# The rest of the modulation summed on VectorE from weights laid out by columns

## The chip, the cores and the metric

The kernel runs on one core of one Trainium2 chip. The metric is the device time of one execution in microseconds (us). Before the change it is 3389.24 us, the median of three runs (3387.71 to 3394.56).

## What is computed

Two transformer-like blocks, all in float32. The first block has two layers over 256 latent and 256 context tokens of width 2048. The layers (`DEPTH` is 2) hold four groups of attention (`oa` to `od`). What the change touches is the modulation at the head of each layer: from two condition vectors `c` and `c_ctx` come a shift, a scale and a gate of 2048 each, by one product with `w_mod[l]` (2048 x 6144).

```python
def first_block(x, c, ctx, c_ctx, w_mod, b_mod, pre_norm_g, w_in, ...):
    silu_c = jax.nn.silu(c)
    silu_cc = jax.nn.silu(c_ctx)
    h, hc = x, ctx
    for l in range(DEPTH):
        with_ctx = l < DEPTH - 1
        shift, scale, gate = jnp.split(silu_c @ w_mod[l] + b_mod[l], 3, axis=-1)
        shift_c, scale_c, gate_c = jnp.split(silu_cc @ w_mod[l] + b_mod[l], 3, axis=-1)
        n = rms_norm(h, pre_norm_g[l]) * (1.0 + scale[:, None]) + shift[:, None]
        nc = rms_norm(hc, pre_norm_g[l]) * (1.0 + scale_c) + shift_c
        p = jnp.split(n @ w_in[l], split_points, axis=-1)
        pc = jnp.split(nc @ w_in[l], split_points, axis=-1)
...
        y = (jnp.concatenate([oa, ob, on, od], axis=-1) * jax.nn.silu(p[12])) @ w_out[l]
        h = h + gate[:, None] * rms_norm(y, post_norm_g[l])
        if with_ctx:
            yc = (jnp.concatenate([oa_c, ob_c, on_c, od_c], axis=-1) * jax.nn.silu(pc[12])) @ w_out[l]
            hc = hc + gate_c * rms_norm(yc, post_norm_g[l])
    return h
```

The second layer needs no gate for the context. The second block (a state-space mixer beside latent attention, then a feed-forward part) is not touched.

## The kernel before

The program is written out by hand: a class `Order` makes one list of steps, and each of the five engines' programs (SyncE, ScalarE, GpSimd, VectorE, TensorE) goes through this list and issues its own part of each step. So every engine works in the order of the list, and semaphores tie the parts together. Nothing is reordered later.

**Projections.** `project` multiplies tiles of 128 tokens by 512 columns of a weight matrix. Weights come in pieces of 128 x 1024 (two slices of 128 rows) through a ring of three on SyncE's queue (line 2409). Each piece is split in two float32r parts: ScalarE copies the high part (`high`, line 1884), VectorE subtracts it for the low part (`low`, line 1227). TensorE makes three products per slice and tile (lines 906 to 908) in `products`. With four token tiles a piece is 24 products; a projection has eight pieces. After each slice and tile of products `side()` is called: one tick of a clock by which other work is put between the products (transposes of heads, one step of attention), and on every fourth tick one step of the background. So a piece has eight ticks and two background steps. The first layer has 1152 ticks.

**Modulation.** The shift and scale of the first layer are made at the start, on TensorE (`mod_products`, line 923, and `mod_turn`), and stay there. The rest, 4 column chunks of 512 of the first layer's gate and 12 of the second layer, is the background generator `modulation()`, and all of it runs during the first layer. For each chunk of 512 columns there are 16 rows of weights, 128 x 512 (256 KB), through a ring `mod_ring` of three. In `mod_row` the partition is the row of the weight matrix:

- VectorE multiplies the row by the activated latent vector's value in the partition and adds it to `mod_acc[0]` (line 1325; line 1321 for the first of a chunk).
- GpSimd does the same for the context with two instructions, a product into `mod_tmp` (line 2304) and an addition to `mod_acc[1]` (line 2306; line 2300 for the first), in the 12 chunks that need the context.
- SyncE loads the row after next as soon as both engines have read the slot (lines 2413, 2414).

After 16 rows `mod_column` on TensorE sums over the partitions with eight products of `mod_acc` by a column of ones (line 943), once both sums are complete, and VectorE adds the bias (line 1332). Only then may both engines start the next chunk. `mod_scale` and `mod_gate` finish the scale and the gate of a layer; the first layer's end waits for its gate and for the second layer's scale.

```python
for i, (l, c, k) in enumerate(todo):
    with_ctx = l < DEPTH - 1 or c < MOD_FIRST
    self.do("mod_row", i, l, c, k, with_ctx)
```

**Heads.** After a projection of queries or keys VectorE (lines 1433 to 1439) and GpSimd (lines 2318 and 2319) rotate them, or ScalarE copies them, and TensorE turns them (line 982). ScalarE takes the exponentials of scores (line 2001), VectorE and ScalarE between them do the rest of softmax. ScalarE and VectorE also make the split features at the head of a layer (lines 1934 to 1940, 1362 and 1370).

Of the kernel before, what the change touches and what calls it, by code (L numbers as in the profile page):

```python
# [13 lines left out]
P = 128  # L14
# [21 lines left out]
MODRING = 3  # L36

# [179 lines left out]
class Order:  # L217
# [90 lines left out]
    def whole(self):  # L308
# [17 lines left out]
        self.do("mod_scale", 0)  # L326
# [13 lines left out]
    def modulation(self):  # L340
        todo = [(0, c, k) for c in range(MOD_FIRST, MODC) for k in range(KT)]
        todo += [(l, c, k) for l in range(1, DEPTH) for c in range(MODC) for k in range(KT)]
        for i in range(MODRING - 1):
            self.do("mod_load", i, *todo[i])
        for i, (l, c, k) in enumerate(todo):
            with_ctx = l < DEPTH - 1 or c < MOD_FIRST
            self.do("mod_row", i, l, c, k, with_ctx)
            if i + MODRING - 1 < len(todo):
                self.do("mod_load", i + MODRING - 1, *todo[i + MODRING - 1])
            yield  # L350
            if k == KT - 1:
                self.do("mod_column", i, l, c, with_ctx)
                if c == MOD_FIRST - 1:
                    self.do("mod_scale", l)
                    self.reached.add(("scale", l))
                if c == MODC - 1:
                    self.do("mod_gate", l)
                    self.reached.add(("gate", l))
                yield
# [339 lines left out]
def build(nc, A, out):  # L699
# [64 lines left out]
    mod_ring = W.two(MODRING, CH)  # L764
    mod_acc = [W.one(CH) for _ in range(2)]
# [6 lines left out]
    mod_tmp = H.one(CH)  # L772
# [115 lines left out]
    def point(event):  # L888
# [3 lines left out]
    products_done, modulation_turned, modulation_summed = (  # L892
        signal(n) for n in ("products_done", "modulation_turned", "modulation_summed"))
# [8 lines left out]
    def tensor_program(e):  # L902
# [32 lines left out]

        def mod_column(i, l, c, with_ctx):
            tb = banks[6]
            for s, n in seen.new(at("mod_lat", i), at("mod_ctx", i) if with_ctx else START, tb.claim("mod_column", l, c)):
                e.wait_ge(s, n)
            for j in range(4):  # L940
                for s in range(2):
                    x = mod_acc[s if with_ctx else 0][:, j * P:(j + 1) * P]
                    done = e.matmul(tb[:, 2 * j + s:2 * j + s + 1], x, ones[:, 0:1], start=True, stop=True)  # L943
            done.then_inc(*modulation_summed.tick(("mod_summed", i // KT)))
# [1644 lines left out]
```

## Time and profile before

| | |
|---|---|
| median of 3 runs | 3389.24 us |
| profiled execution, its own time | 3387.43 us |
| its span | 3385.6 us |
| first layer of the first block | 183 to 1334 us |
| second layer | 1352 to 2059 us |
| granted TensorE clock, mean | 0.929 |
| weight loads of the modulation's rest | 256, 256 KB each |

The span runs from the first to the last instruction of the program. Busy time of an engine leaves out waiting, branching and the issue of DMAs. Matmuls are pipelined and the ends of their records are modelled, so the distance between two starts tells their pace, and the length of a record doesn't. "Idle" lines name the instruction whose completion ended a wait; "issue" means that the profile shows none. In a range "183:1334" the numbers are microseconds from the span's start. The bounds of the layers in the table are those of their first projection and of the update of the stream at their end.

### The profile page before, as it was taken

The numbers are of one execution on the slowest core, as the hardware profiler recorded it, in microseconds if no ns is written. First come the engines' busy times: TensorE is split into PE (matmuls) and PEld (weight loads), VectorE is DVE, ScalarE is ACT, GpSimd is POOL, SyncE is SP. The second block draws the span as 40 slices with busy tenths as digits, with TensorE's granted clock in tenths as the row PEclk, the third lists the DMA queues.
The fourth block names the chain that finished last, engine by engine and source line by source line (L and its number), as shares of the span: only waits on it lengthen the run. The fifth ranks groups of instructions, "written<-read, shape, count | busy, mean of one in ns | idle before, by whom it ended". The sixth has DMA issues, their size and how long they took to land.

```text
span 3385.6 us, 40936 instructions
## 1 busy us (share of the span) xinstructions
PE 3040.6 (90%) x15813; PEld 2449.2 (72%) x15813; DVE 1966.1 (58%) x2774; ACT 1109.5 (33%) x1774; POOL 784.2 (23%) x641
## 2 busy tenths in 40 slices
PE   6789778989978997998998996987999999999998
PEld 1167567777766886767786785764588999999887
DVE  5477876666665544444525455877554666666444
ACT  2132322322312323332423243222343444444443
POOL 0068448577462000000000000655200000000000
PEclk9989889989988999999999997988589899999999
DMA  8844224244333453323333253432033455555655
GB/s 310 279 141 155 75 97 146 97 143 146 110 121 109 171 170 113 116 78 107 108 101 114 78 184 103 142 98 77 14 120 129 141 185 181 186 182 182 197 194 168
DMA packets 148802, 471.19 MB, mean 139 GB/s; under 512 B 16752, under 2 KB 17776, under 8 KB 147440
## 3 DMA queue, kind: packets, MB, share of 16 engines
q1 hardware_dynamic: 137664, 431.03, 38.9%
q10 hardware_dynamic: 8384, 28.63, 2.2%
q0 software_dynamic: 2560, 8.91, 0.8%
q8 instruction: 125, 2.05, 0.2%
q14 instruction: 69, 0.57, 0.1%
HBM read 455.40 MB, written 13.11 MB: 138 GB/s over the span
## 4 chain that ended last, share of the span: by engine, by line
PE 56%; issue 18%; DVE 11%; POOL 7%; DMA 4%; ACT 3%; ACTq 0%; DVEq 0%; POOLq 0%; SPq 0%
PE bank L906 15%; PE bank L907 15%; PE bank L908 15%; POOL first_block_work L2306 3%; DMA common<-w_mod 2%; POOL common L2304 2%; DVE split_weights L1227 2%; PE bank L923 2%; ACT split_weights L1884 1%; DVE first_block_work L1325 1%; PE bank L1020 1%; PE bank L943 1%; PE bank L1098 1%; PE bank L1001 1%; DMA first_block_work<-w_mod_rows 1%
## 5 line engine op out<-in xcount | busy, mean ns | idle before, releaser
L1227 DVE TENSOR_TENSOR split_weights<-common,split_weights 128x1024 fp32r<-128x1024 f32 x628 | 831.5, 1332 | 789.1 <-ACT split_weights L1884 778.5
L1884 ACT ACTIVATE split_weights<-common 128x1024 fp32r<-128x1024 f32 x628 | 656.6, 1053 | 1155.5 <-PE bank L908 1098.0
L906 PE MATMUL bank<-split_weights,features 128*128 128x512 f32 x1920 | 820.6, 427 | 16.3 <-DVE features L1370 10.1
L907 PE MATMUL bank<-split_weights,features 128*128 128x512 f32 x1920 | 770.0, 401 | 0.0
L908 PE MATMUL bank<-split_weights,features 128*128 128x512 f32 x1920 | 769.3, 401 | 0.0
L2276 POOL TENSOR_TENSOR common<-common 128x1 f32<-128x1 f32 (+4 forms) x54 | 39.5, 739 | 1888.6 <-DVE common L1830 752.2
L906 PEld LDWEIGHTS bank<-split_weights,features 128*128 128x128 f32 x1920 | 375.0, 195 | 124.8 <-issue 37.0
L908 PEld LDWEIGHTS bank<-split_weights,features 128*128 128x128 f32 x1920 | 373.3, 194 | 82.7
L907 PEld LDWEIGHTS bank<-split_weights,features 128*128 128x128 f32 x1920 | 374.9, 195 | 79.6 <-issue 11.8
L906 PE MATMUL bank<-ffn_input_split,split_weights 128*128 128x256 f32 (+1 forms) x1376 | 393.1, 286 | 2.8 <-DVE ffn_input_split L1650 1.6
L907 PE MATMUL bank<-ffn_input_split,split_weights 128*128 128x256 f32 (+1 forms) x1376 | 391.6, 285 | 0.0
L908 PE MATMUL bank<-ffn_input_split,split_weights 128*128 128x256 f32 (+1 forms) x1376 | 391.2, 284 | 0.0
L1325 DVE SCALAR_TENSOR_TENSOR first_block_work<-first_block_work 128x512 f32<-128x512 f32 x240 | 283.9, 1183 | 18.9 <-DMA first_block_work<-w_mod_rows 9.5
L2306 POOL TENSOR_TENSOR first_block_work<-first_block_work,common 128x512 f32<-128x512 f32 x180 | 286.3, 1591 | 14.1
L906 PEld LDWEIGHTS bank<-ffn_input_split,split_weights 128*128 128x128 f32 x1376 | 262.4, 191 | 6.6 <-DVE ffn_input_split L1650 2.3
L2304 POOL TENSOR_TENSOR common<-first_block_work 128x512 f32<-128x512 f32 x180 | 236.7, 1315 | 125.8 <-DMA first_block_work<-w_mod_rows 105.6
L908 PEld LDWEIGHTS bank<-ffn_input_split,split_weights 128*128 128x128 f32 x1376 | 263.5, 192 | 0.0
L907 PEld LDWEIGHTS bank<-ffn_input_split,split_weights 128*128 128x128 f32 x1376 | 262.3, 191 | 0.0
L906 PE MATMUL bank<-split_inputs,split_weights 128*128 128x258 f32 (+1 forms) x624 | 196.7, 315 | 4.4 <-DVE split_inputs L1650 3.4
L907 PE MATMUL bank<-split_inputs,split_weights 128*128 128x258 f32 (+1 forms) x624 | 186.4, 299 | 0.0
L908 PE MATMUL bank<-split_inputs,split_weights 128*128 128x258 f32 (+1 forms) x624 | 186.3, 299 | 0.0
L923 PE MATMUL bank<-common,first_block_work 128*2 128x512 f32 x256 | 119.1, 603 | 35.6 <-DMA common<-w_mod 22.9
(282 smaller groups left out, 3677.2 us busy)
## 6 DMA issues: line engine op xcount, KB each, us to landing
common<-w_in SPq DMA_DIRECT2D x252, 512.0 KB, 3.4
common<-w_up SPq DMA_DIRECT2D x172, 512.0 KB, 4.2
first_block_work<-w_mod_rows SPq DMA_DIRECT2D x256, 256.0 KB, 3.6
common<-w_out SPq DMA_DIRECT2D x96, 512.0 KB, 3.3
common<-w_down SPq DMA_DIRECT2D x84, 512.0 KB, 3.3
common<-w_mod SPq DMA_DIRECT2D x64, 512.0 KB, 4.9
trig<-common ACTq DMA_DIRECT2D x32, 272.0 KB, 5.1
second_block_work<-trig POOLq DMA_DIRECT2D x32, 272.0 KB, 3.4
```

Of the source, the lines that this page charges most:

```text
L906: e.matmul(out_ap, xs[0], ws[0], start=first, stop=False)
L907: e.matmul(out_ap, xs[1], ws[0], start=False, stop=False)
L908: return e.matmul(out_ap, xs[0], ws[1], start=False, stop=last)
L923: done = e.matmul(banks[bank][0:2, :], silu_c[:, kk, :], raw_slots[:, m % RAW, k * CH:(k + 1) * CH], start=kk == 0, stop=kk == KT - 1)
L943: done = e.matmul(tb[:, 2 * j + s:2 * j + s + 1], x, ones[:, 0:1], start=True, stop=True)
L1001: e.matmul(sb[:, 0:NT * P - k0], q_t[:, h, t * P:(t + 1) * P], k_t[:, h // (HEADS // kvh), k0:NT * P], start=True, stop=True).then_inc(*sc ...
L1227: e.tensor_tensor(lo, raw, hi.bitcast(F32), ALU.subtract).then_inc(*low_done.tick(("lo", m)))
L1325: e.scalar_tensor_tensor(out=mod_acc[0], in0=w, scalar=x, in1=mod_acc[0], op0=ALU.mult, op1=ALU.add).then_inc(*modulation_added.tick(("mod ...
L1884: e.activation(split_slots[:, 0, i, 0:words], raw_slots[:, m % RAW, 0:words], ACT.Copy).then_inc(*high_done.tick(("high", m)))
L2276: e.tensor_tensor(dst, dst, mh, ALU.pow).then_inc(*powers_done.tick(name))
L2304: e.tensor_tensor(mod_tmp, w, x, ALU.mult).then_inc(*modulation_ctx.tick(("mod_ctx_read", i)))
L2306: e.tensor_tensor(mod_acc[1], mod_acc[1], mod_tmp, ALU.add).then_inc(*modulation_ctx.tick(("mod_ctx", i)))
```

## The change

The weights of the rest of the modulation are laid out by columns (`w_mod_cols`): in a piece the partition is the output column, and along it lie 512 of the 2048 input rows, a quarter. Both condition vectors are laid out along the free axis and repeated over the partitions (`c_rows`, a quarter of both is 128 x 2 x 512). `silu_load` on ScalarE's queue loads a quarter, `silu_row` makes silu of it (tanh on ScalarE, two instructions on VectorE, once for each vector). Then `mod_piece` on VectorE multiplies a piece of weights by the quarter and sums along the free axis in one instruction, `tensor_tensor_reduce`, whose start value is the bias or the sum so far, and whose result is a column of `mod_all`; once for the latents, and once for the context where it is needed. Each such instruction waits for the one before. The first layer's gate goes quarter by quarter (4 x 16 pieces), then the second layer in reversed order of quarters (4 x 48 pieces), seven loads of a quarter in all, since the fourth is kept. There are still 256 pieces of 256 KB, in a ring of three.

`mod_row` (VectorE and GpSimd) and `mod_column` (TensorE and VectorE) are gone.

```diff
     def modulation(self):
-        todo = [(0, c, k) for c in range(MOD_FIRST, MODC) for k in range(KT)]
-        todo += [(l, c, k) for l in range(1, DEPTH) for c in range(MODC) for k in range(KT)]
+        rounds = [(0, q, range(2 * KT, 3 * KT)) for q in range(4)]
+        rounds += [(l, q, range(3 * KT)) for l in range(1, DEPTH) for q in reversed(range(4))]
+        todo = [(l, j, q) for l, q, blocks in rounds for j in blocks]
         for i in range(MODRING - 1):
             self.do("mod_load", i, *todo[i])
...
+        i, row, held = 0, -1, None
+        for l, q, blocks in rounds:
+            if q != held:
+                row, held = row + 1, q
+                self.do("silu_load", row, q, i)
+                yield
+                for s in range(2):
+                    self.do("silu_row", row, s)
+                    yield
+            for j in blocks:
+                first = q == (3 if l else 0)
+                self.do("mod_piece", i, l, j, first, row, l < DEPTH - 1 or j < 2 * KT)
+                if i + MODRING - 1 < len(todo):
+                    self.do("mod_load", i + MODRING - 1, *todo[i + MODRING - 1])
+                i += 1
+                yield
...
+        def mod_piece(i, l, j, first, row, with_ctx):
+            for s, n in seen.new(at("mod_in", i), at("silu_row", row, 1)):
+                e.wait_ge(s, n)
+            for stream in range(2 if with_ctx else 1):
+                total = mod_all[l][:, j, stream:stream + 1]
+                for s, n in seen.new(modulation_added.last()):
+                    e.wait_ge(s, n)
+                e.tensor_tensor_reduce(out=mod_junk, in0=mod_ring[:, i % MODRING, :], in1=silu_rows[:, stream, :], scale=1.0,
+                                       scalar=col("b_mod", l * 3 * KT + j) if first else total, op0=ALU.mult, op1=ALU.add,
+                                       accum_out=total).then_inc(
+                    *modulation_added.tick(*[("mod_read", i)] * (stream == with_ctx)))
...
+        def silu_row(row, stream):
+            words = silu_rows[:, stream, :]
+            for s, n in seen.new(at("silu_row_tanh", row, stream)):
+                e.wait_ge(s, n)
+            e.scalar_tensor_tensor(out=words, in0=mod_junk, scalar=1.0, in1=words, op0=ALU.add, op1=ALU.mult).then_inc(
+                *modulation_scaled.tick())
+            e.wait_ge(*modulation_scaled.last())
+            e.tensor_scalar(words, words, 0.5, None, ALU.mult).then_inc(*modulation_scaled.tick(("silu_row", row, stream)))
...
+        def silu_load(row, q, i):
+            for s, n in seen.new(at("mod_read", i - 1) if i else START):
+                e.wait_ge(s, n)
+            e.dma_start(silu_rows, A["c_rows"][q]).then_inc(*rows_loaded.tick(("c_row", row)))
+
+        def silu_row(row, stream):
+            for s, n in seen.new(at("c_row", row), at("silu_row", row, 0) if stream else START):
+                e.wait_ge(s, n)
+            e.activation(mod_junk, silu_rows[:, stream, :], ACT.Tanh, scale=0.5).then_inc(
+                *tables_made.tick(("silu_row_tanh", row, stream)))
...
-        "w_mod_rows": f["w_mod"].reshape(DEPTH, KT, P, MODC, CH).transpose(0, 3, 1, 2, 4),
+        "w_mod_cols": f["w_mod"].transpose(0, 2, 1).reshape(DEPTH, MOD_BLOCKS, P, 4, QUARTER).transpose(0, 1, 3, 2, 4),
+        "c_rows": np.broadcast_to(np.stack([f["c"][0], f["c_ctx"]]).reshape(2, 4, QUARTER).transpose(1, 0, 2)[:, None],
+                                  (4, P, 2, QUARTER)),
```

The order of instructions on three engines, before and after. First TensorE, in the first layer's first attention (lines 906 to 908 are products of the gate's projection, 992, 1009 and 1020 scores, transposes and values of attention), before:

```order
L992 MATMUL bank<-old_stream 128x512 x2
L906 MATMUL bank<-split_weights,features 128x512
L907 MATMUL bank<-split_weights,features 128x512
L908 MATMUL bank<-split_weights,features 128x512
L943 MATMUL bank<-common,first_block_work 128x1 x8
```

and after, where the same lines are 991, 915 to 917 and 1008:

```order
L991 MATMUL bank<-old_stream 128x512 x2
L915 MATMUL bank<-split_weights,features 128x512
L916 MATMUL bank<-split_weights,features 128x512
L917 MATMUL bank<-split_weights,features 128x512
L1008 MATMUL bank<-common 128x128 x4
```

The block of line 943 is gone from TensorE, here and at 15 other places.

VectorE, between the first two projections of the first layer (1433 to 1439 is the rotation of heads), before:

```order
L1439 TENSOR_TENSOR common<-bank,first_block_work 128x8x32
L1325 SCALAR_TENSOR_TENSOR first_block_work<-first_block_work 128x512 x2
L1227 TENSOR_TENSOR split_weights<-common,split_weights 128x1024
L1332 TENSOR_TENSOR common<-bank,common 128x8
L1321 TENSOR_SCALAR first_block_work<-first_block_work 128x512
```

and after, a little later, where a new quarter comes in:

```order
L1329 ISA common<-first_block_work,common 128x512
L1329 ISA common 128x1
L1226 TENSOR_TENSOR split_weights<-common,split_weights 128x1024
L1317 SCALAR_TENSOR_TENSOR first_block_work<-common,first_block_work 128x512
L1320 TENSOR_SCALAR first_block_work<-first_block_work 128x512
```

Line 1329 is the multiply-and-sum: an instruction over 128x512 and a second one of 128x1 that writes the sum. Each stands 448 times in VectorE's order, 256 for the latents and 192 for the context. Lines 1317 and 1320 are `silu_row`, 14 of each.

ScalarE while features are made (L1946 and L1952 make them), after:

```order
L1885 ACTIVATE split_weights<-common 128x1024
L1928 DMA first_block_work<-c_rows 128x1024
L1933 ACT_TABLE_LOAD
L1933 ACTIVATE common<-first_block_work 128x512
L1946 ACTIVATE common<-bank,common 128x256 x2
```

The load of a quarter and the table load are new at this place; before, the split is followed by the features directly, and the table load stands before the first exponential. Of the seven loads four are followed by the first tanh directly, two after one other instruction, one after four.

## Rows read from the trace of the kernel before

**Rows 1.** The page: engines' busy time, share of the span, instructions.
```profile
PE 3040.6 (90%) x15813; PEld 2449.2 (72%) x15813; DVE 1966.1 (58%) x2774; ACT 1109.5 (33%) x1774; POOL 784.2 (23%) x641
```

**Rows 2.** Stretches: length, busy PE, PEld, DVE, ACT, POOL (count), clock, DMA share, GB/s.
```profile
183.00:1334.00 1151.00, 1023.86 (x4679) 822.27 (x4677) 745.87 (x940) 297.69 (x518) 568.13 (x408) 0.93 0.38 129
1352.00:2059.00 707.00, 654.63 (x2974) 518.91 (x2973) 325.62 (x486) 250.01 (x383) 25.94 (x35) 0.96 0.34 113
...
290.00:400.00 110.00, 90.16 (x402) 68.09 (x403) 79.71 (x106) 27.83 (x48) 70.29 (x50) 0.89 0.34 110
```

**Rows 3.** Waits of TensorE, 183:1334: total us, times, longest.
```profile
PE bank L982 <- POOL first_block_work L2319: 35.6, 12, 5.9
PE bank L943 <- POOL first_block_work L2306: 19.9, 3, 8.7
...
PE bank L943 <- issue: 15.3, 4, 6.1
PE bank L992 <- ACT common L2001: 10.2, 1, 10.2
```

**Rows 4.** Waits of TensorE, 1352:2059.
```profile
PE bank L982 <- POOL first_block_work L2319: 24.7, 11, 5.4
...
PE bank L992 <- ACT common L2001: 1.9, 1, 1.9
```

**Rows 5.** Timeline of TensorE: start us, length us, instruction, count, idle before.
```profile
376.45 1.92 PE L943 MATMUL bank<-common,first_block_work 128*128 128x1 f32 x16
...
956.98 3.55 PE L943 MATMUL bank<-common,first_block_work 128*128 128x1 f32 x16 [8.68 <-POOL first_block_work L2306]
...
961.38 0.63 PE L908 MATMUL bank<-split_weights,features 128*128 128x512 f32 x1
961.81 0.63 PE L906 MATMUL bank<-split_weights,features 128*128 128x512 f32 x1
...
967.11 0.39 PE L908 MATMUL bank<-split_weights,features 128*128 128x512 f32 x1
967.33 0.40 PE L906 MATMUL bank<-split_weights,features 128*128 128x512 f32 x1
```

**Rows 6.** Groups on GpSimd, 183:1334: busy us, mean ns, idle before.
```profile
L2306 POOL TENSOR_TENSOR first_block_work<-first_block_work,common 128x512 f32<-128x512 f32 x180 | 286.3, 1591 | 14.1
L2304 POOL TENSOR_TENSOR common<-first_block_work 128x512 f32<-128x512 f32 x180 | 236.7, 1315 | 125.8 <-DMA first_block_work<-w_mod_rows 105.6 <-POOL first_block_work L2306 0.4
```

**Rows 7.** Groups on VectorE by shape, 183:1334.
```profile
L1325 DVE SCALAR_TENSOR_TENSOR first_block_work<-first_block_work 128x512 f32<-128x512 f32 x240 | 283.9, 1183 | 18.9 <-DMA first_block_work<-w_mod_rows 9.5 <-DVE first_block_work L1325 0.5 <-issue 0.3
L1227 DVE TENSOR_TENSOR split_weights<-common,split_weights 128x1024 fp32r<-128x1024 f32 x143 | 227.1, 1588 | 176.1 <-ACT split_weights L1884 170.7 <-issue 5.2
L1321 DVE TENSOR_SCALAR first_block_work<-first_block_work 128x512 f32<-128x512 f32 x16 | 14.4, 898 | 5.7 <-DMA first_block_work<-w_mod_rows 5.7
...
L1332 DVE TENSOR_TENSOR common<-bank,common 128x8 f32<-128x8 f32 x16 | 2.6, 165 | 60.6 <-PE bank L943 60.6
```

**Rows 8.** Groups on VectorE by shape, 1352:2059.
```profile
L1227 DVE TENSOR_TENSOR split_weights<-common,split_weights 128x1024 fp32r<-128x1024 f32 x144 | 176.1, 1225 | 294.8 <-ACT split_weights L1884 289.9 <-issue 4.9
...
L1471 DVE SCALAR_TENSOR_TENSOR common<-common 128x512 f32<-128x512 f32 x8 | 6.0, 752 | 0.3
...
L1387 DVE TENSOR_TENSOR old_stream<-old_stream,first_block_work 128x512 f32<-128x512 f32 x4 | 2.5, 685 | 0.0
L1455 DVE TENSOR_SCALAR common<-common 128x1 f32<-128x1 f32 x16 | 2.5, 154 | 0.6
```

**Rows 9.** Timeline of VectorE, one instruction waiting for the other.
```profile
376.66 0.49 DVE L1469 TENSOR_SCALAR common<-common 128x512 f32<-128x512 f32 x1
377.18 0.75 DVE L1471 SCALAR_TENSOR_TENSOR common<-common 128x512 f32<-128x512 f32 x1
```

**Rows 10.** Issues of DMAs: queue, count, KB each, median us to landing.
```profile
first_block_work<-w_mod_rows SPq DMA_DIRECT2D x256, 256.0 KB, 3.6
first_block_work<-consts ACTq DMA_DIRECT2D x1, 448.0 KB, 3.8
```

More of the change, by code:

```diff
@@ L36 @@
 MODRING = 3
+MOD_BLOCKS = 3 * KT
+QUARTER = D // 4
 META = 16
@@ L325, in whole @@
             del tables[:TABLES_A_CHUNK]
[L326 removed]
+        self.do("mod_scale", 0, None)
         self.do("tables_end")
@@ L763, in build @@
     silu_c = W.two(KT, 2)
-    mod_ring = W.two(MODRING, CH)
-    mod_acc = [W.one(CH) for _ in range(2)]
+    mod_ring = W.two(MODRING, QUARTER)
+    silu_rows = W.two(2, QUARTER)
     subln = W.one(HD)
@@ L771, in build @@
     probs_t = [H.one(CH) for _ in range(2)]
-    mod_tmp = H.one(CH)
+    mod_junk = H.one(QUARTER)
     lam_words = H.one(4 * SUB)
@@ L934, in mod_turn @@
             done.then_inc(*modulation_turned.tick(*names))
[L936 to L944, printed above, removed]
         def normed_turn(l, f, x):
@@ L1328, in mod_column @@
-        def mod_column(i, l, c, with_ctx):
-            b0 = VEC["b_mod"][0] + l * 3 * KT + 4 * c
-            for s, n in seen.new(at("mod_summed", i // KT)):
-                e.wait_ge(s, n)
-            e.tensor_tensor(mod_all[l][:, 4 * c:4 * c + 4, :], banks[6][:, 0:8].rearrange("p (j s) -> p j s", s=2),
-                            bc(vecs[:, b0:b0 + 4], 2, (P, 4, 2)), ALU.add).then_inc(
-                *modulation_added.tick(("mod_added", l, c), ("free", "mod_column", l, c)))
-        def mod_scale(l):
+            e.scalar_tensor_tensor(out=words, in0=mod_junk, scalar=1.0, in1=words, op0=ALU.add, op1=ALU.mult).then_inc(
+                *modulation_scaled.tick())
@@ L1337, in mod_scale @@
+        def mod_scale(l, i):
             g0 = VEC["pre_g"][0] + l * KT
-            for s, n in seen.new(at("mod_added", l, MOD_FIRST - 1)):
+            for s, n in seen.new(at("mod_added", l, MOD_FIRST - 1) if i is None else at("mod_read", i)):
                 e.wait_ge(s, n)
@@ L1343, in mod_scale, with mod_gate @@
                 *modulation_scaled.tick(("scales_ready", l)))
-        def mod_gate(l):
-            gate = mod_all[l][:, 2 * KT:, :]
-            for s, n in seen.new(at("mod_added", l, MODC - 1)):
+        def mod_gate(l, i):
+            streams = 2 if l < DEPTH - 1 else 1
+            gate = mod_all[l][:, 2 * KT:, 0:streams]
+            for s, n in seen.new(at("mod_read", i)):
                 e.wait_ge(s, n)
-            e.tensor_tensor(gate, gate, bc(vec("post_g")[:, l * KT:(l + 1) * KT], 2, (P, KT, 2)), ALU.mult).then_inc(
+            e.tensor_tensor(gate, gate, bc(vec("post_g")[:, l * KT:(l + 1) * KT], 2, (P, KT, streams)),
+                            ALU.mult).then_inc(
                 *modulation_scaled.tick(("gates_ready", l)))
```

68 lines of the change are left out of this document (16 added, 52 removed).

## Prediction

> **What bounds the kernel now.** Read the table of engine shares first, then stretches of time, then waits. TensorE is busy for 90% of the span, VectorE for 58% [rows 1]. So a microsecond is won or lost where TensorE stands still or runs at its lower clock. The changed work lies in one stretch alone, the first layer of the first block, 183 to 1334 us. The second layer, 1352 to 2059 us, runs the same kinds of projections and attention without modulation or its GpSimd work, and serves as a yardstick. In the first, TensorE is granted 0.93 of 2.4 GHz and GpSimd is busy for 568 us; in the second 0.96, and 26 us [rows 2].
>
> The waits of TensorE in the first layer say what the modulation costs it. It stands 19.9 us before its own modulation products (line 943) for GpSimd's addition (line 2306), 15.3 us more before the same line with no releaser shown, 35.6 us for GpSimd's rotation of heads (line 2319) and 10.2 us once for ACT's exponentials [rows 3]. In the second layer the same rotation costs 24.7 us and the exponentials 1.9 us [rows 4].
>
> Why it waits for GpSimd can be worked out. Plain products start 0.23 us apart at full clock [rows 5]. A piece of weights is 24 of them for four tiles, so 5.5 us, and carries two modulation rows. A group of 16 rows thus passes in 8 pieces, 44 us. GpSimd needs 1.32 + 1.59 = 2.91 us for a row [rows 6], 46.5 us for 16, with rotations beside that. It can't keep up in a plain stretch, and TensorE, in order, stands at the end of the group until the last row is summed: 8.68 us in the case shown [rows 5].
>
> **The change part by part.** My sum is made against the profiled execution: 3387.4 us, a span of 3385.6 and 1.8 around it; the median of the three runs, 3389.2, is 1.8 above it.
>
> *Removed from TensorE.* 16 blocks of line 943. One takes 1.92 us at full clock, 3.55 at the lower one [rows 5]; at 1.92 they are 31 us. The waits before them, 19.9 + 15.3 [rows 3], go too, since nothing of the new modulation is on TensorE: 35 us. Together **-66**. If another wait came straight in their place only the 31 would go; with every block at 3.55 us it would be -92.
>
> *Removed from GpSimd.* All 192 rows. The rotation then finds it free, as in the second layer: 35.6 - 24.7 = **-11** [rows 3, 4]. The one long wait for exponentials stood behind VectorE's slow consts; I take it down to the second layer's: 10.2 - 1.9 = **-8**. Both could be 0 if VectorE is as late as GpSimd was.
>
> *The clock.* Fewer and shorter stops leave the clock at its 2.4 GHz level longer. After the long stop at 957 us the products first ran at the lower level, 0.43 us apart. I take the mean from 0.93 to 0.95, short of the second layer's 0.96 [rows 2]. On a stretch of about 1065 us that is 1065 x 0.02/0.95 = **-22**; the bounds are 0 (no change) and -33 (0.96).
>
> *VectorE.* It loses 240 + 16 row instructions, 283.9 + 14.4 us, and 16 additions, 2.6 us; it also gets back what its splits lost beside GpSimd: 143 x (1.588 - 1.225) = 52 us [rows 7, 8]. From 745.9 us in the stretch [rows 2] 393 are left. It gains 448 multiply-and-sum instructions, each with a second one that writes the sum, and each waiting for the one before. The trace has no such pair. The nearest row is a product of two float32 tensors in SBUF, 128x512, 685 ns (line 1387). The second part is nearest to the 128x1 instruction, 154 ns [rows 8]. A dependent instruction follows 0.03 us after the end of the one before (376.66 + 0.49 to 377.18) [rows 9]. So 0.87 us each, 390 us. The 14 halves of the activated input rows take 0.75 + 0.49 us each [rows 8, 9], 17 us. VectorE then has 393 + 390 + 17 = 800 us in some 1065: 75%, against 65% now. That hides beside TensorE on the mean. In a plain stretch it is tight: per piece one split of 1.23 and four sums of 0.87, 4.7 of 5.5 us. Splits, rotations and softmax steps now queue behind 1.74 us of sums at a time, where it was one row of 1.2. Some will be late. The share of 79.7/110 that VectorE already has in an attention stretch [rows 2] went without TensorE waiting long for splits. I put **+15** for this; 0 at least, and 60 where all plain stretches run at VectorE's pace. The bounds of the pair itself are 0.69 us (the second part hidden in the first) and 1.55 us (below).
>
> By a rule of the Trainium skill the pair would be dearer: "DVE Microarchitecture Reference", Points that are easy to get wrong, says that a form with two inputs from SBUF that aren't bf16 has half the throughput, since no read port is left for the accumulator. By the row the sum has 390 us of VectorE, by the rule about 1.4 us each, over 600 us; what that would do is the second rival.
>
> *ACT and the queues.* Seven loads of 512 KB and 14 tanh. In ACT's order the load is followed by its tanh, in four of seven cases with nothing between and in two with one instruction, so ACT stands for the landing: 3.8 us for the load nearest in size on its queue [rows 10]. Behind it in order are splits of weights, features, exponentials. ACT is busy only 297.7 of 1151 us [rows 2], and splits are made ahead of use, so most is hidden: **+12**, between 0 and 7 x 4 = 28. The first load also lies in the stretch where features are made, where a table load precedes the first tanh; that one isn't new, it only moves from the first exponential. SP issues the same 256 loads of 256 KB; they are released by VectorE alone now, no longer by GpSimd. Counted in the program's order, the last piece of modulation comes at tick 1112 of the layer's 1152 ticks, 24 later than before, so the layer's end doesn't wait. Other stages are untouched: 0.
>
> Sum: -66 - 11 - 8 - 22 + 15 + 12 = **-80**, so 3387.4 - 80 = 3307.
>
> **The rivals.**
>
> *VectorE's sums are dearer than the row, but not double.* A piece has 5.5 us; less the split and 0.3 for heads, four sums fill it at 1.0 us each. At 1.15 us a piece takes 6.1, 0.6 too much, on the three quarters of 144 pieces that carry both streams: 108 x 0.6 = +65 in place of my +15. Time 3357. For it: the form isn't in the trace. Against: every float32 row of 512 words lies at 0.68 to 0.75 us.
>
> *The sums take twice the row.* 2 x 0.685 + 0.15 + 0.03 = 1.55 us, 448 of them 694 us; VectorE has 393 + 694 + 17 = 1104 us of work and becomes the bound in every stretch of the layer, since TensorE needs each split from it. At a 90% share, more than any stretch shows now, the layer takes 1227 us in place of 1151: **3463**, slower. It decides from (0.9 x 1151 - 410)/448 = 1.4 us on. Against: line 1471 reads two float32 tensors from SBUF and a scalar at 752 ns [rows 8], one pass. For: it writes no accumulator. The rule named above is this rival.
>
> *The waits only change their name.* TensorE loses 66 us at line 943, but heads, features and splits queue longer behind sums and behind ACT's landings, 60 + 28 us, and the clock stays. That is 3387.4 - 66 - 19 + 88 = **3390**. Against: VectorE's mean load stays below that of a bound engine. For: VectorE alone now carries what two engines did.
>
> **How the numbers follow.** About 7 us, 0.2%, is what a measurement of this kernel can tell from no change. The forecast, with all its terms between their bounds, gets 0.72 (of it 0.04 below 3268, where the clock and the stops give all they can: -92 - 19 - 33 = -144 at the very most, 3243). Dearer sums get 0.13, changed names 0.05, the double price 0.10. Faster: 0.72 + 0.13 = 0.85; same: 0.05; slower: 0.10. The range leaves out the 0.04 below, the 0.10 of the double price and the 0.05 of changed names, 0.19 in all: 3268 to 3380.
>
> **What would show it.** In the profile after: no line for modulation on TensorE or GpSimd; TensorE's idle time in the first layer down by some 50 us and its clock at 0.95; the split of weights at 1.23 us in both layers; the sums at 0.69 us and their second part at 0.15 or less; VectorE near 75% busy between 183 and some 1255 us, where the first layer ends. ACT shows waits for the input rows of up to 4 us, seven times. I am wrong if the main part of a sum takes over 1 us, if waits for splits, which are not among TensorE's long ones now, grow past 30 us, or if the clock doesn't move.

## The result and the profile after

The changed kernel takes 3252.7 us in the median (3250.3 to 3255.1, four runs), the kernel before 3388.5 us in the same comparison. The ratio is 0.960, 95% interval 0.958 to 0.962: 136 us faster. The direction was forecast; the 80 us that were forecast were too few, and the time lies below the range of 3268 to 3380.

The update of the stream that ends a layer says where the time went. Before, the first of these updates began at 1336.5 us, in the first layer, and the last at 2059.1, in the second. The row for the instruction of line 1582 in the trace after (minimum, median, maximum length, first and last start):

```profile
L1582 DVE SCALAR_TENSOR_TENSOR old_stream<-first_block_work,common,old_stream x6: 2342/2344/2352, 1201.7 to 1922.4; 128x2048 f32<-128x2048 f32 x6
```

The first layer ends 134.8 us sooner and the second 136.7; the whole profiled execution is 137.1 us shorter, so what follows the first layer has its old length within some 2 us. Engine shares after, from the page:

```profile
PE 2958.3 (91%) x15557; PEld 2384.8 (73%) x15557; DVE 1950.4 (60%) x3426; ACT 1118.0 (34%) x1788; POOL 247.4 (8%) x269
```

The two layers as stretches, with the columns of [rows 2]:

```profile
183.00:1199.00 1016.00, 945.77 (x4424) 760.90 (x4422) 726.20 (x1585) 303.45 (x529) 31.23 (x36) 0.98 0.44 149
...
1217.00:1924.00 707.00, 650.30 (x2974) 516.64 (x2974) 327.22 (x487) 250.13 (x383) 26.21 (x35) 0.96 0.34 113
```

Read against [rows 2], the first layer can be split in three. TensorE's idle time falls from 1151 - 1024 = 127 us to 1016 - 946 = 70, by 57. A lower clock costs time only while TensorE is busy. So its busy time times the shortfall of its granted clock from full speed was summed over stretches of 0.5 us of the same traces: 65 us before and 18 after, 47 less. What is left of the busy time is the work as it would last at full speed: 959 us before and 928 after, 31 less, as long as the 16 blocks of 1.92 us. Together this is the 135 us. So a good third of the gain is the clock, to which the prediction gave a quarter. The mean clocks of the rows, 0.07 and 0.02 short over the whole length, would make it 60 us, but they count the idle time too.

TensorE's waits, 183 to 1199 us, beside [rows 3]:

```profile
PE bank L981 <- POOL first_block_work L2314: 29.4, 12, 5.4
PE bank L1008 <- DVE common L1471: 16.4, 7, 4.4
PE bank L1008 <- DVE common L1510: 6.5, 5, 2.3
PE bank L991 <- ACT common L2013: 4.8, 1, 4.8
```

No wait for modulation is left. The rotation costs 29.4 us where it cost 35.6, the exponentials 4.8 where they cost 10.2. VectorE's groups, to be read beside [rows 7] and [rows 8]:

```profile
L1329 DVE CUSTOM_DVE_ANT_0 common<-first_block_work,common 128x512 f32<-128x512 f32 x448 | 338.1, 755 | 22.3 <-DMA first_block_work<-w_mod_cols 1.6 <-issue 0.3
L1226 DVE TENSOR_TENSOR split_weights<-common,split_weights 128x1024 fp32r<-128x1024 f32 x142 | 173.9, 1225 | 135.8 <-ACT split_weights L1885 74.6 <-issue 61.1
L1329 DVE DVE_READ_ACCUMULATOR2_ANT common<- 128x1 f32 x448 | 36.9, 82 | 0.0
```

The split takes 1225 ns in the first layer too. A sum takes 755 ns, its second part 82, and the two overlap, as VectorE's timeline shows:

```profile
500.14 0.75 DVE L1329 CUSTOM_DVE_ANT_0 common<-first_block_work,common 128x512 f32<-128x512 f32 x1
500.82 0.08 DVE L1329 DVE_READ_ACCUMULATOR2_ANT common<- 128x1 f32 x1
500.94 0.75 DVE L1329 CUSTOM_DVE_ANT_0 common<-first_block_work,common 128x512 f32<-128x512 f32 x1
```

From one sum to the next, with the wait between them, it is 0.80 us, where 0.87 was put.

### The profile page after: what moved, and what is told of

The parts are those of the page before. It is cut to its first block, busy times and chain, and to the rows that moved or that the text cites. A ratio compares the mean times of both kernels' runs of the same rounds, so it can differ in the third digit from the quotient of the medians.

```text
span 3248.5 us, 40339 instructions
## 1 busy us (share of the span) xinstructions
PE 2958.3 (91%) x15557; PEld 2384.8 (73%) x15557; DVE 1950.4 (60%) x3426; ACT 1118.0 (34%) x1788; POOL 247.4 (8%) x269
## 4 chain that ended last, share of the span: by engine, by line
PE 53%; issue 29%; DVE 9%; DMA 3%; POOL 2%; ACT 2%; ACTq 0%; DVEq 0%; POOLq 0%
PE bank L915 15%; PE bank L916 14%; PE bank L917 14%; DMA common<-w_mod 2%; PE bank L932 2%; PE bank L1097 1%; DVE split_weights L1226 1%; POOL common L2288 1%; PE bank L1019 1%; PE bank L1160 1%; PE bank L1112 1%; ACT split_weights L1885 1%; POOL first_block_work L2313 1%; PE bank L1000 1%; PE bank L1104 1%
## 5 line engine op out<-in xcount | busy, mean ns | idle before, releaser
L1226 DVE TENSOR_TENSOR split_weights<-common,split_weights 128x1024 fp32r<-128x1024 f32 x628 | 779.4, 1249 | 746.7 <-ACT split_weights L1885 680.6
L915 PE MATMUL bank<-split_weights,features 128*128 128x512 f32 x1920 | 803.6, 419 | 7.9 <-DVE features L1370 3.4
L917 PE MATMUL bank<-split_weights,features 128*128 128x512 f32 x1920 | 757.7, 395 | 0.0
L916 PE MATMUL bank<-split_weights,features 128*128 128x512 f32 x1920 | 757.3, 394 | 0.0
L915 PEld LDWEIGHTS bank<-split_weights,features 128*128 128x128 f32 x1920 | 366.5, 191 | 107.9 <-issue 30.9
L916 PEld LDWEIGHTS bank<-split_weights,features 128*128 128x128 f32 x1920 | 367.0, 191 | 77.9 <-issue 11.5
L917 PEld LDWEIGHTS bank<-split_weights,features 128*128 128x128 f32 x1920 | 365.7, 190 | 79.3
L1329 DVE CUSTOM_DVE_ANT_0 common<-first_block_work,common 128x512 f32<-128x512 f32 x448 | 338.1, 755 | 22.3 <-DMA first_block_work<-w_mod_cols 1.6
L915 PEld LDWEIGHTS bank<-split_inputs,split_weights 128*128 128x128 f32 x624 | 126.7, 203 | 17.2 <-issue 13.1
L915 PE MATMUL bank<-split_weights,gated_split 128*128 128x512 f32 x344 | 134.1, 390 | 0.0
```

The costliest lines, as they stand in the source:

```text
L915: e.matmul(out_ap, xs[0], ws[0], start=first, stop=False)
L916: e.matmul(out_ap, xs[1], ws[0], start=False, stop=False)
L917: return e.matmul(out_ap, xs[0], ws[1], start=False, stop=last)
L1226: e.tensor_tensor(lo, raw, hi.bitcast(F32), ALU.subtract).then_inc(*low_done.tick(("lo", m)))
L1329: e.tensor_tensor_reduce(out=mod_junk, in0=mod_ring[:, i % MODRING, :], in1=silu_rows[:, stream, :], scale=1.0, scalar=col("b_mod", l * 3 ...
```

## The experiments

Two theories. **S** (stops): the gain is TensorE's blocks, the waits before them and the lower clock after them. **P** (port): the gain is that VectorE's instructions are no longer slowed beside GpSimd's; the runs can show the slowing, not what makes it. The times of the kernel before in the four comparisons are 3392.9, 3391.6, 3389.7 and 3390.1 us; each ratio is taken to the one of its own comparison. The changed kernel's 3252.7 us come from a fifth, with 3388.5, so a difference in times from it can be off by up to 5 us; where this matters, the difference by the ratios is given too.

The first layer of each kernel, split in three as above (estimates from one profile each, in us):

| kernel | first layer | idle | lost to the clock | work at full speed |
|---|---|---|---|---|
| before | 1151 | 127 | 65 | 959 |
| changed | 1016 | 70 | 18 | 928 |
| before, without GpSimd's rows | 1039 | 57 | 23 | 959 |
| before, without blocks | 1079 | 110 | 40 | 929 |
| before, without either | 1003 | 56 | 20 | 927 |
| changed, with blocks put back | 1061 | 70 | 34 | 957 |
| changed, short stops | 1071 | 104 | 32 | 935 |
| changed, long stops | 1141 | 151 | 57 | 933 |
| without blocks, rotation on VectorE | 1066 | 104 | 33 | 929 |
| the same, without GpSimd's rows | 994 | 50 | 16 | 928 |

### A square: GpSimd's rows and TensorE's blocks, one, the other, both away

Without GpSimd's rows (its function `mod_row` is gone), TensorE's blocks take the latent sum alone:

```diff
-            for s, n in seen.new(at("mod_lat", i), at("mod_ctx", i) if with_ctx else START, tb.claim("mod_column", l, c)):
+            for s, n in seen.new(at("mod_lat", i), tb.claim("mod_column", l, c)):
...
-                    x = mod_acc[s if with_ctx else 0][:, j * P:(j + 1) * P]
+                    x = mod_acc[0][:, j * P:(j + 1) * P]
```

Without the blocks (TensorE's function `mod_column` is gone), VectorE adds the bias to the first columns of the row sums, and at a new chunk of columns VectorE and GpSimd each wait for their own last chunk alone, no longer for TensorE:

```diff
-            for s, n in seen.new(at("mod_summed", i // KT)):
+            for s, n in seen.new(at("mod_lat", i)):
...
-            e.tensor_tensor(mod_all[l][:, 4 * c:4 * c + 4, :], banks[6][:, 0:8].rearrange("p (j s) -> p j s", s=2),
+            e.tensor_tensor(mod_all[l][:, 4 * c:4 * c + 4, :], mod_acc[0][:, 0:8].rearrange("p (j s) -> p j s", s=2),
```

The third kernel has both edits.

> The kernel before with GpSimd's rows left out (the context's modulation isn't computed; TensorE's 16 blocks sum the latent rows for both). Theory S (stops: the gain was TensorE's blocks, the waits before them and the lower clock after them): the waits for GpSimd at line 943 and with no releaser (35 us) go, the blocks of 1.92 us stay, the clock of the first layer rises to about 0.96: 3285 us, 30 above the changed kernel. Theory P (port: the gain was that GpSimd no longer slows VectorE's instructions): splits at 1.23 us and no gain left over, so 3255, like the changed kernel.

> The kernel before without the 16 blocks on TensorE (the sum over the partitions is left out; VectorE takes its bias addition from the accumulator), with all rows on VectorE and GpSimd kept. Theory S: nothing stops TensorE for the modulation though GpSimd is as late as before; 66 us of blocks and waits and some 45 us of clock go: 3280 us. Theory P: splits still take 1.59 us on average beside GpSimd, so little is gained: 3360.

> The kernel before without GpSimd's rows and without TensorE's blocks: only VectorE's 256 rows are left (context and sum over partitions aren't computed). Both theories: all gains of the change and less work on VectorE, 3240 us. With the two runs above it makes a square: theory S expects that taking the blocks away is worth 110 us with GpSimd's rows there and 45 without them, theory P that it is worth under 40 in both.

Measured, with 3392.9 us for the kernel before: 3274.1 us without GpSimd's rows (ratio 0.9651, 0.9636 to 0.9665), 3309.2 without the blocks (0.9755, 0.9741 to 0.977), 3235.1 without either (0.9536, 0.9521 to 0.955). The first layer of each, columns as in [rows 2]; first without GpSimd's rows:

```profile
183.00:1222.00 1039.00, 981.71 (x4686) 794.17 (x4684) 565.88 (x940) 298.49 (x519) 29.89 (x36) 0.97 0.42 143
```

without the blocks:

```profile
183.00:1262.00 1079.00, 968.78 (x4424) 774.79 (x4423) 771.01 (x940) 298.58 (x518) 579.03 (x408) 0.95 0.41 138
```

without either:

```profile
183.00:1186.00 1003.00, 946.92 (x4423) 761.23 (x4422) 565.35 (x940) 298.05 (x518) 29.88 (x36) 0.97 0.43 148
```

The blocks are worth 84 us with GpSimd's rows there and 39 without them; GpSimd's rows 119 us with the blocks and 74 without. So theory S is right in that the two share some 45 us, which only the two together cost, as the stops of TensorE for the last row of a group do. But 74 us of GpSimd's rows have nothing to do with the blocks (54 of idle time and 20 of clock by the table), and S has no place for them: 3280 was expected without blocks, 3309 came. Theory P falls on the same corner, 84 us where it allowed 40. Without GpSimd's rows 3274 lies between the 3285 of S and the 3255 of P, and without either 3235 is near the 3240 of both. Neither theory holds alone. VectorE is busy for 771 us in the layer with GpSimd's rows and for 565 without, for the same 940 instructions.

The changed kernel stands 18 us above the kernel without either (3252.7 and 3235.1), 22 by the ratios. That is the whole price of doing the context on VectorE, with its input rows: 726 us of VectorE in place of 565.

### How GpSimd's rows cost 74 us without a block to wait for them

TensorE's waits without the blocks, 183 to 1180 us, show the likeliest way: the rotation of heads (line 2309 there) stands behind the rows in GpSimd's queue.

```profile
PE bank L972 <- POOL first_block_work L2309: 46.4, 11, 10.9
```

So the end of the rotation was moved to VectorE, and GpSimd's function for it taken away, in both kernels without blocks, with and without GpSimd's rows.

```diff
+            dst = halves(rows_buf[r % 2][:, 0:w], half)
+            for s, n in seen.new(at("turned_sin", r), point(order.row_before[r])):
+                e.wait_ge(s, n)
+            e.tensor_tensor(dst[:, :, 0, :], a[:, :, 0, :], b[:, :, 0, :], ALU.subtract).then_inc(*heads_made.tick())
+            e.tensor_tensor(dst[:, :, 1, :], a[:, :, 1, :], b[:, :, 1, :], ALU.add).then_inc(
+                *heads_made.tick(("rotated", r), ("turn", x)))
```

> The kernel before without TensorE's blocks and with the end of the rotation on VectorE, so that almost nothing of TensorE's waits for GpSimd, which still makes all its rows beside VectorE. Beside the run with blocks away and nothing else (3309), and its fellow without GpSimd's rows. Theory L (GpSimd's rows cost 74 us there because the rotation stands behind them): 20 to 30 us over the fellow, 3255. Theory P (they cost because they slow VectorE, whose splits take 1.6 in place of 1.23 us): 60 or more over the fellow, 3290.

> The fellow: the kernel before without blocks, without GpSimd's rows, with the end of the rotation on VectorE. Both theories: 3235 less the 12 us that the rotation on VectorE gave the changed kernel, 3223.

Measured: 3292.4 us (ratio 0.972, 0.9689 to 0.9752) with GpSimd's rows and 3219.5 (0.9504, 0.9472 to 0.9536) without. Theory P's 3290 and the fellow's 3223 came out. The difference is 73 us, as large as the 74 before the rotation was moved. So it is not the rotation standing behind the rows that costs. The powers for the norms of heads are still GpSimd's, but VectorE waits about as long for them (line 1403, 183 to 1180 us): 8.9 us with the rows, 7.7 without. With the rows, VectorE's two largest groups, its first rows of a chunk and TensorE's longest wait, 183 to 1180 us:

```profile
L1315 DVE SCALAR_TENSOR_TENSOR first_block_work<-first_block_work 128x512 f32<-128x512 f32 x232 | 279.0, 1202 | 36.8 <-DMA first_block_work<-w_mod_rows 29.4
L1217 DVE TENSOR_TENSOR split_weights<-common,split_weights 128x1024 fp32r<-128x1024 f32 x131 | 226.0, 1725 | 74.5 <-ACT split_weights L1880 68.3 <-issue 6.1
...
L1311 DVE TENSOR_SCALAR first_block_work<-first_block_work 128x512 f32<-128x512 f32 x16 | 14.0, 873 | 6.6 <-DMA first_block_work<-w_mod_rows 6.0
```

```profile
PE bank L972 <- DVE first_block_work L1434: 40.0, 11, 10.2
```

and without them:

```profile
L1315 DVE SCALAR_TENSOR_TENSOR first_block_work<-first_block_work 128x512 f32<-128x512 f32 x240 | 179.5, 748 | 12.8 <-DMA first_block_work<-w_mod_rows 3.8
L1217 DVE TENSOR_TENSOR split_weights<-common,split_weights 128x1024 fp32r<-128x1024 f32 x143 | 175.1, 1225 | 272.9 <-ACT split_weights L1880 266.1 <-issue 6.8
...
L1311 DVE TENSOR_SCALAR first_block_work<-first_block_work 128x512 f32<-128x512 f32 x16 | 7.7, 482 | 6.4 <-DMA first_block_work<-w_mod_rows 5.9
```

```profile
PE bank L972 <- DVE first_block_work L1434: 17.6, 11, 4.7
```

Beside GpSimd's rows VectorE's row takes 1202 ns and not 748, its split 1725 and not 1225. The first row of a chunk, which reads one tensor, goes from 482 to 873. These are averages of two lengths. In the timelines of the same profile with GpSimd's rows, among the instructions that stand by themselves, those that ran wholly beside one of GpSimd's rows and those that met none last 1.47 and 0.75 us for a row (44 and 42 of them), 2.04 and 1.23 us for a split (69 and 57). For line 1552, which reads one operand from PSUM, it is 0.67 and 0.68 us (10 and 6). VectorE also waits 29.4 us for loads, against 3.8, since a slot of the ring comes free with the later of its two readers; so GpSimd's lateness may still cost by this way. TensorE then waits for the rotation on VectorE itself, 40 us against 17.6. So what GpSimd's rows cost, VectorE pays first. How much of the 73 us is the slower instructions and how much the late loads isn't told apart.

### The blocks alone, put back into the changed kernel

```diff
                 i += 1
                 yield
+                if i % KT == 0:
+                    self.do("ones_block", i)
+                    yield
...
+        def ones_block(i):
+            tb = banks[6]
+            for s, n in seen.new(tb.claim("ones_block", i)):
+                e.wait_ge(s, n)
+            for j in range(8):
+                done = e.matmul(tb[:, j:j + 1], ident, ones[:, 0:1], start=True, stop=True)
+            done.then_inc(*modulation_turned.tick(("free", "ones_block", i)))
```

> The changed kernel with 16 blocks of eight one-column products put back on TensorE, which wait for nothing of the modulation. Theory S: 16 x 1.9 = 30 us, and little of the clock, since a block alone is no stop: 3285. If the blocks themselves pull the clock down, the clock of the first layer falls from 0.98 to 0.95 and it is 3310. Theory P: 3255.

Measured: 3293.9 us (0.9707, 0.9691 to 0.9724), 41 above the changed kernel, 37 by the ratios, which agrees with the 39 of the square. It lies between the two numbers expected. The first layer:

```profile
183.00:1244.00 1061.00, 991.23 (x4683) 801.69 (x4681) 726.84 (x1582) 304.05 (x531) 31.20 (x36) 0.96 0.42 143
```

TensorE is idle for 70 us, as without the blocks. By the table it has 29 us more of work and loses 16 more to the clock. So blocks without any stop cost their own 30 us and about 16 of clock in this one profile; by the times, 37 to 41 in all, some 10 of clock.

### Stops without work, short and long

TensorE does one one-column product at the same 16 places and waits until GpSimd has made 5 (STOP_OPS), or 15, 128x1 products.

```diff
+        def stop(i):
...
+            e.matmul(tb[:, 0:1], ident, ones[:, 0:1], start=True, stop=True).then_inc(
+                *modulation_turned.tick(("stop_reached", i), ("free", "stop", i)))
+            for s, n in seen.new(at("stop_over", i)):
+                e.wait_ge(s, n)
...
+            for k in range(STOP_OPS):
+                e.tensor_tensor(spare[:, 1:2], ones[:, 0:1], ones[:, 1:2], ALU.mult).then_inc(
+                    *powers_done.tick(*[("stop_over", i)] * (k == STOP_OPS - 1)))
+                e.wait_ge(*powers_done.last())
```

> The changed kernel with 16 pure stops of TensorE, at the places where the blocks stood: one one-column product, then TensorE waits until GpSimd has done five 128x1 products after it. If the lower clock follows stops (theory S), the time grows by the length of the stops and by some 5 us more for each, about 16 x 2 to 4 us and 40 to 80 us of clock, and the profile shows 10 us at the lower clock behind each: 3340 to 3390. If the lower clock had another cause (the blocks' small products, the load of VectorE), the time grows by the stops alone: 3290 to 3310.

> The changed kernel with 16 stops of fifteen GpSimd products, about 6 us each, three times those of the run before (which stopped TensorE for about 2 us each, 34 us in all, and put 65 us more of the first layer at the lower clock, half of that lost). If long stops cost 5 us of clock each, as the 10 us behind the long waits of line 943 say: 96 + 80 us, 3430. If a stop costs the same 2 us of clock whatever its length: 96 + 32, 3380.

Measured: 3302.3 us with short stops (0.9733, 0.9718 to 0.9747), 3372.5 with long ones (0.9955, 0.994 to 0.9969). The first layer with short stops:

```profile
183.00:1254.00 1071.00, 967.10 (x4459) 776.03 (x4458) 725.85 (x1581) 303.96 (x531) 55.39 (x116) 0.96 0.41 142
```

and with long ones:

```profile
183.00:1324.00 1141.00, 989.88 (x4461) 793.10 (x4459) 727.13 (x1583) 303.79 (x531) 94.35 (x276) 0.93 0.39 133
```

Short stops add 104 - 70 = 34 us of idle time, 2.1 each, and by the table 14 us of clock, 0.9 each. Long ones add 151 - 70 = 81 us of idle time, 5.1 each, and 39 us of clock, 2.4 each. The rest, 5 to 7 us, is the small products. The expected 5 us per stop was too much for both, and a stop doesn't cost the same whatever its length: in this kernel a microsecond of stop takes some 0.4 to 0.5 us more through the clock at either length. The times say the same: 50 and 120 us above the changed kernel (45 and 121 by the ratios), for 34 and 81 us of idle time. The 3302 us alone don't decide between the theories, for they lie in the range of 3290 to 3310 that was set for stops without a price in clock; the granted clock of the layer, 0.96 in place of 0.98, does.

### How much more VectorE can carry

Sums made a second time into a spare column, only the latent ones (the edit below) or, without its condition, all 448.

```diff
+                if stream == 0:
+                    e.tensor_tensor_reduce(out=mod_junk, in0=mod_ring[:, i % MODRING, :], in1=silu_rows[:, stream, :], scale=1.0,
+                                           scalar=col("b_mod", l * 3 * KT + j), op0=ALU.mult, op1=ALU.add,
+                                           accum_out=spare[:, 0:1]).then_inc(*modulation_added.tick())
```

> The changed kernel with each of the 256 latent sums made twice (the first into a spare column): 205 us more of VectorE, 931 of 1016 us in the first layer. Theory H (VectorE's work is hidden as long as a plain piece fits: one split and the sums, 1.23 + 6 x 0.80 = 6.0 us against 5.5): 0.5 us too much on each of 96 pieces, 50 us, 3300. Theory Q (every late queue costs as GpSimd's did, from well below its limit): over 80 us, 3335 and more.

> The changed kernel with all 448 sums made twice, so a sum costs 1.6 us, the price of the prediction's rival of the double row: VectorE has 726 + 358 = 1084 us for the first layer and bounds it. By the rival's arithmetic (a share of 0.9 at most) the layer takes 1204 us in place of 1016, 3440; if VectorE, once it is the bound, is busy to 0.97, 1118 us, 3355.

Measured: 3320.1 us (0.9784, 0.9769 to 0.9798) and 3466.3 (1.0214, 1.0197 to 1.0231). The first layer with 256 more sums, then with 448 more:

```profile
183.00:1270.00 1087.00, 969.29 (x4434) 774.47 (x4433) 915.72 (x2101) 304.10 (x531) 31.22 (x36) 0.95 0.42 140
```

```profile
183.00:1417.00 1234.00, 994.52 (x4430) 782.66 (x4428) 1059.53 (x2483) 302.85 (x529) 31.22 (x36) 0.91 0.37 123
```

All 448 sums made twice cost more than the 3440 expected. Together with the kernel without either, which has rows in place of sums, this is a curve: VectorE busy for 565 us of the layer, 3235 us; 726, 3253; 916, 3320; 1060, 3466. The first 161 us of work cost 18 (22 by the ratios), the next 190 cost 67 (63), the last 144 cost 146: each microsecond of VectorE's work is then one of time, at a share of 1060/1234 = 0.86. The 67 us lie between the two theories' numbers. With all sums doubled TensorE waits for splits, which it hardly did before, but longer still for heads (183 to 1200 us):

```profile
PE bank L982 <- POOL first_block_work L2320: 88.8, 11, 17.5
PE bank L916 <- DVE split_weights L1227: 29.2, 19, 1.8
```

This kernel also has what the prediction's rival of the double row described, a sum of 1.6 us. The rival's time was 3463 us; it is 3466. That is partly luck: the rival had 1104 us of work at a share of 0.90, and it is 1060 at 0.86.

### The input rows loaded once

```diff
+                if row:
+                    for s in range(3):
+                        yield
+                else:
                     self.do("silu_load", row, q, i)
```

> The changed kernel with the quarter of the input rows loaded and activated once, not seven times (all pieces are multiplied by the first quarter; the pieces keep their places). It shows what six loads on ACT's queue, twelve tanh and 24 instructions on VectorE cost. Prediction's term: 6/7 of 12 us, 3242. Theory H: hidden, 3252.

All later pieces wait for the first quarter alone. Measured: 3246.8 us (0.957, 0.9556 to 0.9585), 6 under the changed kernel, 10 by the ratios; the intervals of the two ratios touch, so that this is hardly more than no difference. The wait of ACT for the rows in the changed kernel (us, times), from the row on line 1933:

```profile
  DMA first_block_work<-c_rows: 14.3, 5
```

It stands for the landing five times, 2.9 us each, and most of it is hidden.

### Shorter waits for heads

The longest wait left is TensorE's for the rotation. Its end on VectorE, as in the edit above; the transposes one tick later; both:

```diff
-            self.turned.append((self.clock + 3, ("turn_heads", l, g, part, nh, t, r)))
+            self.turned.append((self.clock + 4, ("turn_heads", l, g, part, nh, t, r)))
```

> The changed kernel with the subtraction and addition of the rotated heads on VectorE (685 and 350 ns rows) in place of GpSimd (870 and 750 ns and a hand-over each way). The longest wait that is left, 29 us in the first layer and some 25 in the second. Stops theory: 12 + 12 stops shorter by about 1 us each and less clock: 3230. If TensorE's wait is for VectorE being late anyway, the work only moves: 3253.

> The changed kernel with the transposes of heads one tick (0.69 us of products) later in TensorE's order. The wait of each is shorter by up to 0.69 us, 24 x 0.69 = 16 us and as much of clock: 3225. If the buffers of rotated rows come free too late for it (two of them, one tile every two ticks), ACT and VectorE wait instead and nothing is won: 3253.

> Both of the two before in one kernel. If they add up: 3205 to 3215; if one has taken the wait away already, the better of the two.

Measured: 3240.9 us (0.9565, 0.9551 to 0.9579), 3245.2 (0.9576, 0.9555 to 0.9596) and 3232.1 (0.9542, 0.9526 to 0.9558). The first gave 12 us where 23 were expected, the second 8 where 28 were, and its interval overlaps that of the changed kernel (0.958 to 0.962). Together they give 21, about their sum, but miss the 3205 to 3215 expected; it is the fastest of the kernels that compute everything. In it TensorE still waits for heads (line 981), 183 to 1190 us:

```profile
PE bank L981 <- ACT old_stream L2004: 12.1, 6, 4.2
PE bank L981 <- DVE first_block_work L1444: 10.9, 8, 4.0
```

Part of the wait has moved to ACT, which copies the turned heads.

## Why the prediction was wrong in size

**What bounds, and where.** Right: the whole gain lies in the first layer, and TensorE there stood for GpSimd's rows. The arithmetic of 2.91 us a row, two to a piece, against the 5.5 us of a piece [rows 5, 6] stands.

**Removed from TensorE, -66.** Right as far as the runs tell it. The blocks' own work is 31 us by the table. Alone they cost 37 to 41 us with their part of the clock, and 84 beside GpSimd's rows, which also holds the waits for those.

**Removed from GpSimd, -11 and -8.** The two waits fell by 6 and 5. Features and the turned probabilities gave some more; all idle time fell by 57 us, where -35 - 11 - 8 = -54 was put for it. But the prediction then set +27 against this, for VectorE and ACT, and no such idle time appeared.

**The clock, -22.** This step failed. The level of the second layer was taken as a mark, 0.95 on the way to 0.96, with -33 as the bound. It became 0.98, and the stretch gave back 47 us. The second layer is no bound, for it has stops of its own, 707 - 655 = 52 us of idle time [rows 2]; the clock should have been costed by the stops and blocks that went. The long stops of 81 us in the experiment took 39 us of clock; by that rate of 0.5, the 57 us of idle time that went are worth some 28, and the blocks, which took 10 to 16 without a stop, come on top, so that some 40 were to be had.

**VectorE, +15.** This step failed too, in its sign. The 52 us that splits get back without GpSimd's rows were booked as busy time and then hidden, and the greater load was made a cost against the kernel before. The pair of runs with the rotation on VectorE shows GpSimd's rows to cost 73 us through VectorE. Nor was it the splits alone: every row of 748 ns took 1202 there, and without blocks VectorE was busy for 771 us with GpSimd's rows and 565 without. So the changed kernel makes 448 passes over weights on VectorE where it made 256, in less busy time: 726 us where it was 746 and where 800 were put. Against the right mark, a kernel that has neither, the whole new load costs 18 to 22 us, and the term of +15 has about that size.

**ACT, +12.** Measured 6 to 10 for six of the seven loads, hardly clear of nothing: a term of 7 to 12, within its bounds.

**The rivals.** The double row did not come; its time was right to 3 us, by two errors that cancel. A sum of 1.26 us on average (256 of 448 made twice, 0.80 x 704/448) gives 3320, where the rival of dearer sums had 3357 at 1.15; by its arithmetic 1.26 would give some 3406. Most of these 86 us too many are the terms that it shares with the forecast, and some 30 its way of pricing each plain piece beyond 5.5 us in full. Of the Trainium skill ("Vector Engine (DVE) Microarchitecture Reference", Points that are easy to get wrong) the rule of half the throughput, with two inputs from SBUF that aren't bf16, names one form, `S2S2D2_STT`. The profile calls the sum CUSTOM_DVE_ANT_0, and it isn't halved: 755 ns for 512 float32 elements from two tensors, beside 685 for the plain product [rows 8]. No run has the form that the page names with its accumulator.

The sum with what was measured: -57 of idle time, -47 of clock and -31 of work make -135 for the first layer. The forecast had -54, -22 and -31, and +27 for VectorE and ACT. So of the 55 us that it missed, 25 are the clock, 27 the waits that were added and did not come, and 3 the idle time. The prediction gave 0.04 to a time below 3268.

## What to carry to other kernels

When an engine in the background shares its tiles or its time with one that feeds TensorE, look first at what its neighbour's instructions last with and without it: here moving work from GpSimd to VectorE unburdened VectorE. Cost a stop of TensorE together with the clock that it takes, by stops of the same kernel and not by the mean clock of another stretch. And let a curve of three or four loads tell what an engine off the critical path can carry: some 20 us for the first 161 us of work here, 146 for the last 144.

## What was not expected of the hardware

- VectorE's instructions with two inputs in SBUF are slower beside GpSimd's rows: 1202 in place of 748 ns for a row of 512, 1725 in place of 1225 ns for a split of 1024, on average over a layer, and 1.47 and 2.04 us where the whole instruction ran beside one. An instruction with one input from SBUF, the first row of a chunk, is slower too, 873 in place of 482 ns. One that reads its second operand from PSUM (line 1552) keeps its 0.67 us.
- The multiply-and-sum over 512 float32 elements takes 755 ns, and the instruction that writes its sum overlaps it: 0.80 us from one to the next.
- Sixteen blocks of eight one-column products on TensorE, some 30 us of work without a stop, lowered the granted clock of the layer from 0.98 to 0.96. Stops of 2.1 and of 5.1 us took 0.4 to 0.5 us through the clock for each microsecond of stop.
